# Four narrow projections with the activations moving: 8 or 24 output columns as the stationary operand, turned afterwards

## The chip, the cores and the metric

One core of a Trainium2 chip runs the whole program. The metric is the device time in microseconds of one execution; the figure for a kernel is the median of its runs.

## The reference, cut to what matters

The reference is a stack of three blocks on 512 tokens of width 1024, in fp32. Four of its layers begin with one wide input projection of the normed activations, `u = x @ w_in`, whose columns are then cut into parts: queries, keys, values, gates, and, among them, a few very narrow parts. The narrow ones are the subject here:

- Even layer, `ba`: 8 columns, beta and the decay of a gated delta rule for 4 heads
- Odd layer (here called Fox), `f`: 8 columns, the forget gate of 8 heads
- Second block, `dt` of its state space part (Ssd): 8 columns
- Second block, `gl` of its sparse attention part (Nsa): 24 columns, 3 gates for each of 8 heads

Each is needed with tokens on the partitions: as [128 tokens, 4 token tiles, 8 or 24], that is, 512 x 8 or 512 x 24.

## The kernel before

Activations lie feature-major: 8 tiles of [128 features x 512 tokens], each as a high and a low fp32r half (`Split`), so that a product is three matmuls: high by high, high by low, low by high (`three`, L278). Weights are cut into pieces (`Weights.piece`). SyncE loads them in groups of one or two neighbouring pieces into three raw slots; the load of a group waits until the pieces of the group three places before it have been split. ScalarE copies a piece's high half (`Weights.act`), VectorE subtracts for its low half (`Weights.dve`). Both are called with the key of the piece in use and run one piece ahead: the call for a piece splits also the one that follows in TensorE's order, even where that one belongs to the next layer. The high half of a piece waits until TensorE has finished with the piece two before it.

Two forms of product use a piece. `tile` (L283) keeps 128 (or fewer) weight columns stationary and moves 512 tokens: 8 feature tiles x 3 = 24 matmuls into one PSUM bank, the result with output columns on the partitions. `lin_tm` (L316) keeps 128 tokens of X stationary and moves the weight's columns: for each of 4 token tiles 24 matmuls, so 96, into four banks, the result with tokens on the partitions. The four narrow projections use `lin_tm`. For every matmul there is one load of the stationary operand.

Each engine's order of work is written out by hand. All engines meet at `fence` at the start of a norm and between the stages. `K.rinv`, a [128 x 512] scratch tile, holds a norm's 1/rms and is free once the norm has run.

What stands around the four places:

- Even: 12 qkv tiles, 4 z tiles, `ba`, 8 rope tiles (each followed by one fp32 matmul with the rotation, which waits for ScalarE's copy of the tile), dv. After its split for `ba` ScalarE issues the DMA of the positions (L1091). VectorE copies the four parts of `ba` as they finish, waits for the positions, computes angles for sine and cosine (`rope_tables_dve`), ScalarE applies Sin, and only then copies the first rope tile.
- Fox: the norm, `f` as the first product, 8 q tiles, 8 k tiles, v, 8 gate tiles; `f` is used by VectorE after the gate tiles. The layer ahead of it, `Ple`, ends with 8 proj tiles; for the last of them VectorE calls `G.dve`, which splits the first piece of Fox, and then multiplies and adds the tile into x. The fence of Fox's norm follows.
- Ssd: after a fence `dt`, 8 x tiles (each: ScalarE's copy, a convolution of 4 operations on VectorE, Silu on ScalarE, before ScalarE splits the weights two tiles on), z.
- Nsa: q, k and v tiles, `gl`, on which ScalarE runs a Sigmoid for each of 4 parts, 4 ga tiles with Silu on ScalarE, then the matmuls of a compression (hid) whose results take a Silu too. ScalarE's split call for the last ga tile comes ahead of that tile's Silu and includes the first weights of the output product.

The lines of the helpers in the profile: L90 a matmul, L93 a transpose, L87 a copy, L83 an activation, L96 a tensor_tensor, L99 a tensor_scalar, L102 a scalar_tensor_tensor, L76 the wait in a fence, L255 a weight load's issue.

Of the kernel before, what the change touches and what calls it, by code (L numbers as in the profile page):

```python
# [8 lines left out]
ACT = mybir.ActivationFunctionType  # L9
# [8 lines left out]
    {"ev_pad": 12, "ev_padz": 3, "ev_conv": 12, "ev_qkv": 12, "ev_z": 4, "ev_ba": 4, "ev_y": 1, "ev_na": 1, "ev_beta": 1,  # L18
     "ev_rope": 8, "ev_dv": 4},
# [6 lines left out]
    {"fox_f": 4, "fox_q": 8, "fox_k": 8, "fox_va": 4, "fox_vd": 4, "fox_g": 8, "fox_y": 2, "fox_zero": 5, "fox_lf": 2,  # L26
     "fox_cum": 2},
# [161 lines left out]
class Weights:  # L189
# [453 lines left out]
class Net:  # L643
# [154 lines left out]
def blocks(ap, a):  # L798
    return ap.rearrange("p (a b) -> p a b", a=a)
# [108 lines left out]
class Even:  # L908
# [164 lines left out]
    def act(self, act):  # L1073
        K, G, S = self.K, self.K.G, self.K.S
# [15 lines left out]
        G.act(act, ("even.ba", 0, 0))  # L1090
# [11 lines left out]
        act.wait_ge("ev_ba", 4)  # L1102
# [63 lines left out]
    def dve(self, dve):  # L1166
        K, G, S = self.K, self.K.G, self.K.S
        self.norm.dve(dve)
        cw = K.pv("conv_w")
        for n in range(12):  # L1170
            G.dve(dve, ("even.qkv", n))
            dve.wait_ge("ev_pad", n + 1)
            b, q = self.pads[n % 3], self.qkv[:, n, :]
            dve.own(dve.ts(q, b[:, 0:T], cw[:, n:n + 1], None, MUL, None))
            for j in range(1, 4):
                dve.settle()
                t = dve.stt(q, b[:, j:j + T], cw[:, j * 12 + n:j * 12 + n + 1], q, MUL, ADD)
# [5 lines left out]
        G.dve(dve, ("even.ba", 0, 0))  # L1183
# [15 lines left out]
        dve.wait_ge("ev_ba", 4)  # L1199
# [530 lines left out]
class Fox:  # L1730
# [22 lines left out]
    def pe(self, pe):  # L1753
# [89 lines left out]
    def dve(self, dve):  # L1843
        K, G, S = self.K, self.K.G, self.K.S
        self.norm.dve(dve)
        G.dve(dve, ("fox.f", 0, 0))
        for tt in range(4):
            k = ("fox.f", 0, tt)
            dve.wait_ge("mm", K.done[k])
            dve.cp(self.f[:, tt, :], G.at[k]).then_inc(S("fox_f"), 1)  # L1850
        for n in range(8):
            G.dve(dve, ("fox.q", n))
        for n in range(8):
            k = ("fox.k", n)
# [12 lines left out]
        dve.wait_ge("fox_f", 4)  # L1867
# [79 lines left out]
class Second:  # L1947
# [270 lines left out]
    def ssd_dve(self, dve):  # L2218
# [3 lines left out]
        G.dve(dve, ("ssd.dt", 0, 0))  # L2222
        for tt in range(4):
            k = ("ssd.dt", 0, tt)
            dve.wait_ge("mm", K.done[k])
            dve.cp(self.dt[:, tt, :], G.at[k]).then_inc(S("ssd_dt"), 1)
# [13 lines left out]
        dve.wait_ge("ssd_dt", 4)  # L2240
# [87 lines left out]
class Nsa:  # L2328
# [52 lines left out]
    def pe(self, pe):  # L2381
# [112 lines left out]
    def act(self, act):  # L2494
# [31 lines left out]
        G.act(act, ("nsa.gl", 0, 0))  # L2526
        for tt in range(4):
# [39 lines left out]
    def dve(self, dve):  # L2567
# [29 lines left out]
        G.dve(dve, ("nsa.gl", 0, 0))  # L2597
# [1032 lines left out]
```

## Time and profile before

| | |
|---|---|
| median of 3 runs | 3948.49 us (3943.27 to 3951.49) |
| profiled execution | 3948.09 us, span 3945.8 us |
| mean granted TensorE clock | 0.922 |
| TensorE matmul busy | 3501.7 us, 89% of the span |
| TensorE weight load busy | 2729.1 us, 69% |
| VectorE, ScalarE, GpSimd busy | 52%, 33%, 9% |

The span is the stretch that the profiler's instructions cover; the execution's own time is 2.3 us more. TensorE's busy time is no measure of its speed: matmuls are pipelined, and a matmul that runs at half clock or that waits for its stationary operand's load counts as busy too. The granted clock is given as a share of 2.4 GHz.

### The profile page before, as it was taken

To read this page: it belongs to the slowest core of one execution; us is meant where nothing else is said; L and a number is where in the kernel's file an instruction comes from. 1 tells how busy PE (TensorE), PEld (TensorE's weight loads), DVE (VectorE), ACT (ScalarE), POOL (GpSimd) and SP (SyncE) were. 2 spreads that over 40 slices of the span, in tenths; PEclk is the share of its full clock that TensorE was granted. 3 is DMA by queue.
4 is the path that set the end of the run, shared out by engine and by line. 5 is a ranking of instruction groups with operands and counts; after the bars stand their busy time and mean duration, and the time that the engine had idled before them with its cause. 6 is when DMAs were issued, how large, how long until landed. Compare 5 with 4: busy or idle time off the path is not lost.

```text
span 3945.8 us, 51140 instructions
## 1 busy us (share of the span) xinstructions
PE 3501.7 (89%) x21050; PEld 2729.1 (69%) x21050; DVE 2040.2 (52%) x3597; ACT 1293.1 (33%) x2131; POOL 366.5 (9%) x338
## 2 busy tenths in 40 slices
PE   6977889999899999997797889868888889998998
PEld 4745867777686677775676676546677777776886
DVE  5434446664422456654445425558766773445443
ACT  3222133222222332223333124345455442423321
POOL 0000200000000000000001000025443330000000
PEclk9876989999799999999887989989899989999999
DMA  4210013442343034432201220021111102232321
GB/s 137 59 43 0 1 59 97 138 145 82 64 80 80 24 99 128 139 103 84 91 27 38 60 76 16 27 75 50 36 36 36 47 18 75 65 118 75 97 96 64
DMA packets 318855, 274.93 MB, mean 70 GB/s; under 512 B 10913, under 2 KB 310049, under 8 KB 317857
## 3 DMA queue, kind: packets, MB, share of 16 engines
q1 hardware_dynamic: 314368, 256.07, 22.0%
q10 hardware_dynamic: 4256, 15.59, 1.1%
q8 instruction: 169, 2.77, 0.3%
q14 instruction: 62, 0.50, 0.0%
HBM read 265.35 MB, written 6.29 MB: 69 GB/s over the span
## 4 chain that ended last, share of the span: by engine, by line
PE 75%; DVE 14%; ACT 5%; issue 3%; POOL 1%; DMA 1%; DVEq 0%; ACTq 0%; SPq 0%; POOLq 0%
PE ps L90 73%; DVE f L102 5%; DVE f L96 3%; DVE r L96 2%; ACT f L83 2%; PE ps L93 2%; DVE f L99 2%; DVE f L108 1%; POOL f L96 1%; ACT f L87 1%; ACT r L87 1%; ACT L83 1%; ACT f L84 1%; DVE f L105 0%; DVE f L3173 0%
## 5 line engine op out<-in xcount | busy, mean ns | idle before, releaser
L90 PE MATMUL ps<-r,r 128*128 128x512 f32 (+2 forms) x10656 | 2527.6, 396 | 146.6 <-DVE r L96 100.8
L90 PEld LDWEIGHTS ps<-r,r 128*128 128x128 f32 x10656 | 2003.4, 196 | 624.8 <-issue 192.9
L90 PE MATMUL ps<-f,f 64*64 64x64 f32 (+10 forms) x9458 | 908.9, 283 | 221.3 <-DVE f L96 51.3
L90 PEld LDWEIGHTS ps<-f,f 64*64 64x64 f32 (+4 forms) x9458 | 643.1, 163 | 471.6 <-issue 248.3
L96 DVE TENSOR_TENSOR r<-f,r 128x1024 fp32r<-128x1024 f32 (+2 forms) x619 | 654.1, 1063 | 497.6 <-ACT r L87 490.1
L87 ACT ACTIVATE r<-f 128x1024 fp32r<-128x1024 f32 (+2 forms) x548 | 507.1, 938 | 851.4 <-PE ps L90 715.0
L87 ACT ACTIVATE f<-ps 128x512 f32<-128x512 f32 (+3 forms) x410 | 182.2, 459 | 655.0 <-PE ps L90 416.1
L102 DVE SCALAR_TENSOR_TENSOR f<-f,f,f 128x128 f32<-128x128 f32 (+3 forms) x622 | 362.0, 588 | 41.6 <-ACT f L83 25.6
L96 POOL TENSOR_TENSOR f<-f,f 128x512 f32<-128x512 f32 (+2 forms) x280 | 322.6, 1165 | 517.7 <-ACT f L83 293.3
L96 DVE TENSOR_TENSOR f<-ps,f 128x512 f32<-128x512 f32 (+4 forms) x325 | 178.1, 561 | 330.0 <-PE ps L90 322.3
L83 ACT ACTIVATE f<-ps 128x512 f32<-128x512 f32 (+4 forms) x206 | 112.3, 547 | 658.3 <-PE ps L90 656.4
L96 DVE TENSOR_TENSOR f<-f,f 128x256 f32<-128x256 f32 (+5 forms) x372 | 221.3, 607 | 18.9 <-ACT f L83 10.1
L96 POOL TENSOR_TENSOR r<-f,r 128x512 fp32r<-128x512 f32 (+1 forms) x25 | 38.4, 1537 | 2005.8 <-ACT r L87 2005.8
L96 DVE TENSOR_TENSOR f<-f 128x512 f32<-128x512 f32 x129 | 86.9, 687 | 229.7 <-ACT f L83 217.6
L108 DVE RECIPROCAL f<-f 128x1 f32<-128x1 f32 (+4 forms) x193 | 72.3, 382 | 211.7 <-ACT f L83 105.6
L83 ACT ACTIVATE f<-f 128x512 f32<-128x512 f32 (+8 forms) x206 | 100.3, 514 | 201.3 <-DVE f L102 86.5
L93 PE MATMUL ps<-f,f 128*128 128x128 f32 x552 | 109.3, 319 | 62.4 <-DVE f L102 26.7
L96 DVE TENSOR_TENSOR f<-f,ps 128x512 f32<-128x512 f32 (+1 forms) x192 | 110.8, 594 | 77.5 <-PE ps L90 66.2
L93 PEld LDWEIGHTS ps<-f,f 128*128 128x128 f32 x552 | 72.0, 159 | 86.3 <-DVE f L102 31.8
L87 DVE COPY f<-ps 128x256 f32<-128x256 f32 (+8 forms) x106 | 43.3, 410 | 163.2 <-PE ps L90 156.5
L83 ACT ACT_TABLE_LOAD x89 | 114.2, 1283 | 31.1 <-DVE f L105 18.1
L83 ACT ACTIVATE f<-f,f 128x512 f32<-128x512 f32 (+2 forms) x165 | 109.5, 705 | 14.8 <-POOL f L96 13.9
(32 smaller groups left out, 726.7 us busy)
## 6 DMA issues: line engine op xcount, KB each, us to landing
f<-in_w_mlp_up SPq DMA_DIRECT2D x32, 1024.0 KB, 6.5
f<-in_w_mlp_down SPq DMA_DIRECT2D x32, 1024.0 KB, 6.6
f<-in_w_ff SPq DMA_DIRECT2D x32, 1024.0 KB, 5.3
f<-in_w_ada SPq DMA_DIRECT2D x48, 512.0 KB, 4.1
f<-in_w_in SPq DMA_DIRECT2D x24, 1024.0 KB, 5.3
f<-in_w_in SPq DMA_DIRECT2D x44, 512.0 KB, 3.8
f<-in_w_in_even SPq DMA_DIRECT2D x12, 1024.0 KB, 5.7
f<-in_w_in_odd SPq DMA_DIRECT2D x12, 1024.0 KB, 11.2
```

Of the source, the lines that this page charges most:

```text
L83: return self.e.activation(out, in_, func, bias=bias, scale=scale)
L84: return self.e.activation(out, in_, func, bias=bias, scale=scale, accum_out=acc)
L87: return self.e.activation(out, in_, ACT.Copy) if self.name == "act" else self.e.tensor_copy(out, in_)
L90: return self.e.matmul(out, l, r, start=first, stop=last)
L93: return self.e.transpose(out, in_, ident)
L96: return self.e.tensor_tensor(out, a, b, op)
L99: return self.e.tensor_scalar(out, a, s1, None, o0) if o1 is None else self.e.tensor_scalar(out, a, s1, s2, o0, o1)
L102: return self.e.scalar_tensor_tensor(out=out, in0=a, scalar=s, in1=b, op0=o0, op1=o1)
L108: return self.e.reciprocal(out, in_)
```

## The change

Each of the four narrow projections becomes one `tile` of 24 matmuls with its 8 or 24 weight columns stationary and the 512 tokens moving. The result lies as [8 x 512] or [24 x 512] in one PSUM bank. ScalarE copies it to rows 0 to 7 (0 to 23) of `K.rinv`. TensorE then turns it with four transposes into one bank ([128 x 4 x 8]), and one copy on VectorE (for `gl` one Sigmoid on ScalarE) takes that to its place in SBUF. The transposes are placed behind the tile that follows (for Even behind the first rope tile and its rotation).

Three things move: in Even the DMA of the positions stands behind ScalarE's new wait for the product and its copy; in Fox `f` stands between the q and the k tiles, where it was first; in Nsa the Sigmoid stands behind the four Silus of ga. The counts of semaphores follow.

```diff
+    def turned(self, pe, key, m, landed, drained):
+        K = self.K
+        pe.wait_ge(*landed)
+        b = K.ps.take(pe, drained)
+        for tt in range(4):
+            t = pe.tr(K.ps.t[b][:, tt * m:tt * m + m], K.rinv[0:m, tt * 128:tt * 128 + 128], K.ident[0:m, 0:m])
+        K.mm_done(t, key)
+        return b
...
@@ Even, pe
-        G.lin_tm(pe, "even.ba", W, 2048, 8, X, lambda tt, b: [("ev_ba", tt + 1)])
+        G.tile(pe, "even.ba", W, 2048, 8, X, [("ev_bar", 1)])
         for i in range(8):
             G.tile(pe, ("even.rope", i), ...)
             self.rope.pe(pe, i)
+            if i == 0:
+                self.bank["ba"] = G.turned(pe, "even.baT", 8, ("ev_bar", 1), ("ev_ba", 1))
@@ Even, act
-        G.act(act, ("even.ba", 0, 0))
+        G.act(act, "even.ba")
+        act.wait_ge("mm", K.done["even.ba"])
+        act.cp(K.rinv[0:8, :], G.at["even.ba"]).then_inc(S("ev_bar"), 1)
         act.e.dma_start(self.pos_i, K.A["positions"][0].partition_broadcast(128)).then_inc(S("d_pos"), 16)
@@ Even, dve
-        for tt in range(4):
-            dve.wait_ge("mm", K.done["even.ba", 0, tt])
-            dve.cp(self.ba[:, tt, :], G.at["even.ba", 0, tt]).then_inc(S("ev_ba"), 1)
         dve.wait_ge("d_pos", 16)
...
         for i in range(8):
             G.dve(dve, ("even.rope", i))
+            if i == 0:
+                dve.wait_ge("mm", K.done["even.baT"])
+                dve.cp(self.ba, blocks(K.ps.t[self.bank["ba"]][:, 0:32], 4)).then_inc(S("ev_ba"), 1)
             self.rope.dve(dve, i, ...)
@@ Fox, pe (act and dve follow it)
-        G.lin_tm(pe, "fox.f", W, 4096, 8, X, lambda tt, b: [("fox_f", tt + 1)])
         for n in range(8):
             G.tile(pe, ("fox.q", n), W, n * 128, 128, X, [("fox_q", n + 1)])
+        G.tile(pe, "fox.f", W, 4096, 8, X, [("fox_fr", 1)])
         for n in range(8):
             G.tile(pe, ("fox.k", n), W, 1024 + n * 128, 128, X, [("fox_k", n + 1)])
+            if n == 0:
+                self.bank["f"] = G.turned(pe, "fox.fT", 8, ("fox_fr", 1), ("fox_f", 1))
@@ Ssd, pe (act copies to rinv, dve copies dt at n == 1)
-        G.lin_tm(pe, "ssd.dt", W, 3352, 8, X, lambda tt, b: [("ssd_dt", tt + 1)])
+        G.tile(pe, "ssd.dt", W, 3352, 8, X, [("ssd_dr", 1)])
         for n in range(8):
             G.tile(pe, ("ssd.x", n), ...)
+            if n == 0:
+                self.bank["dt"] = G.turned(pe, "ssd.dtT", 8, ("ssd_dr", 1), ("ssd_dt", 1))
@@ Nsa, pe
-        G.lin_tm(pe, "nsa.gl", W, 1280, 24, X, lambda tt, b: [("nsa_gl", tt + 1)])
+        G.tile(pe, "nsa.gl", W, 1280, 24, X, [("nsa_glr", 1)])
         for n in range(4):
             G.tile(pe, ("nsa.ga", n), ...)
+            if n == 0:
+                self.bank["gl"] = G.turned(pe, "nsa.glT", 24, ("nsa_glr", 1), ("nsa_gl", 1))
@@ Nsa, act
-        for tt in range(4):
-            k = ("nsa.gl", 0, tt)
-            act.wait_ge("mm", K.done[k])
-            act.f(self.gl[:, tt, :], G.at[k], ACT.Sigmoid).then_inc(S("nsa_gl"), 1)
+        act.wait_ge("mm", K.done["nsa.gl"])
+        act.cp(K.rinv[0:24, :], G.at["nsa.gl"]).then_inc(S("nsa_glr"), 1)
         for n in range(4):
             ...
             act.f(self.ga[:, n, :], G.at[k], ACT.Silu).then_inc(S("nsa_ga"), 1)
+        act.wait_ge("mm", K.done["nsa.glT"])
+        act.f(self.gl, blocks(K.ps.t[self.bank["gl"]][:, 0:96], 4), ACT.Sigmoid).then_inc(S("nsa_gl"), 1)
```

## Rows read from the trace of the kernel before

**Rows 1.** The page: the chain of work that ended last, by engine

```profile
PE 75%; DVE 14%; ACT 5%; issue 3%; POOL 1%; DMA 1%; DVEq 0%; ACTq 0%; SPq 0%; POOLq 0%
```

**Rows 2.** Groups by form (busy us, mean ns), two of TensorE, and the page's transposes

```profile
L90 PE MATMUL ps<-r,r 128*128 128x512 f32 x9984 | 2417.9, 401 | 121.8 <-DVE r L96 87.1 <-DVEq L76 17.2 <-ACT r L83 7.2
...
L90 PE MATMUL ps<-r,r 128*128 128x8 f32 x288 | 55.4, 329 | 11.0 <-ACT r L87 9.5 <-DVEq L76 0.9 <-POOL r L96 0.7
...
L93 PE MATMUL ps<-f,f 128*128 128x128 f32 x552 | 109.3, 319 | 62.4 <-DVE f L102 26.7
```

**Rows 3.** Windows, Even: stretch, length, busy and count by engine, granted clock, DMA

```profile
136.03:138.70 2.67, 2.67 (x26) 2.67 (x25) 1.09 (x1) 1.54 (x2) 0.00 (x0) 1.00 0.39 119
...
146.51:151.63 5.12, 5.12 (x25) 5.12 (x26) 0.17 (x1) 0.00 (x0) 0.00 (x0) 0.50 0.00 0
```

**Rows 4.** Timeline, Even: start us, duration, instruction, idle before and releaser

```profile
136.04 0.33 ACTq L1091 DMA_DIRECT2D f<-in_positions  x1
...
151.72 0.42 DVE L87 CAST f<-f 128x512 f32<-128x512 int32 x1
...
162.72 2.07 PE L90 MATMUL ps<-f,f 128*128 128x512 f32 x2 [4.08 <-ACT f L87]
```

**Rows 5.** The positions' two DMAs, from issue to landing

```profile
DMA to landing us min/median/max: 3.1/3.2/3.3
```

**Rows 6.** Timeline at the end of the layer ahead of Fox

```profile
1026.31 97.69 SPq L255 DMA_DIRECT2D f<-in_w_in_odd  x9
...
1029.93 0.26 ACT L87 ACTIVATE r<-f 128x64 fp32r<-128x64 f32 x1 [1.35 <-PE ps L90]
...
1032.40 0.69 DVE L96 TENSOR_TENSOR f<-f,f 128x512 f32<-128x512 f32 x1
```

**Rows 7.** DMA issues, last column landing us; issued near 1028, 1031 and 1080

```profile
f<-in_w_in_odd SPq DMA_DIRECT2D x1, 1024.0 KB, 11.8
...
f<-in_w_in_odd SPq DMA_DIRECT2D x1, 1024.0 KB, 19.7
...
f<-in_w_in_odd SPq DMA_DIRECT2D x1, 1024.0 KB, 8.6
```

**Rows 8.** Timeline at the end of the second such layer: split of the next piece

```profile
1855.62 1.06 ACT L87 ACTIVATE r<-f 128x1024 fp32r<-128x1024 f32 x1 [2.97 <-DMA f<-in_w_mem_kv]
1856.71 1.23 DVE L96 TENSOR_TENSOR r<-f,r 128x1024 fp32r<-128x1024 f32 x1 [1.45 <-ACT r L87]
```

**Rows 9.** Timeline, Fox: last part of X reaches TensorE, and the first read of q0

```profile
1058.47 66.78 PE L90 MATMUL ps<-r,r 128*128 128x8 f32 x287 [0.32 <-POOL r L96]
...
1082.67 0.60 ACT L83 ACTIVATE f<-ps 128x512 f32<-128x512 f32 x1 [6.97 <-PE ps L90]
```

**Rows 10.** Windows, Fox: the second quarter of f, and the tile q1

```profile
1059.33:1064.40 5.07, 5.07 (x25) 5.07 (x26) 0.15 (x3) 0.00 (x0) 1.17 (x3) 0.50 0.01 3
...
1082.67:1088.11 5.44, 5.44 (x25) 4.50 (x24) 1.23 (x1) 1.55 (x2) 0.00 (x0) 1.00 0.35 73
```

**Rows 11.** Timeline, Ssd: start of dt, read of x0, start of x2

```profile
2002.10 31.59 PE L90 MATMUL ps<-r,r 128*128 128x8 f32 x144 [0.88 <-DVEq L76]
...
2028.28 0.60 ACT L87 ACTIVATE f<-ps 128x512 f32<-128x512 f32 x1 [6.83 <-PE ps L90]
...
2034.84 11.38 PE L90 MATMUL ps<-r,r 128*128 128x512 f32 x48 [1.16 <-DVE r L96]
```

**Rows 12.** Nsa: v's last read, window of ga0, table load, wait for output weights

```profile
2267.56 0.28 ACT L87 ACTIVATE f<-ps 128x128 f32<-128x128 f32 x1 [5.08 <-PE ps L90]
...
2284.74:2291.93 7.19, 7.19 (x25) 5.79 (x26) 1.23 (x1) 2.42 (x3) 0.00 (x0) 0.77 0.45 144
...
2285.90 1.28 ACT L83 ACT_TABLE_LOAD   x1
...
2322.01 1.06 ACT L87 ACTIVATE r<-f 128x1024 fp32r<-128x1024 f32 x1 [18.60 <-DMA f<-in_w_out]
```

**Rows 13.** Window in the head norms: 8 stationary, 512 moving columns, fp32

```profile
252.00:254.00 2.00, 2.00 (x5) 0.19 (x4) 0.00 (x0) 1.45 (x3) 0.00 (x0) 1.00 0.00 0
```

More of the change, by code:

```diff
@@ L17 @@
 STAGES = (
-    {"ev_pad": 12, "ev_padz": 3, "ev_conv": 12, "ev_qkv": 12, "ev_z": 4, "ev_ba": 4, "ev_y": 1, "ev_na": 1, "ev_beta": 1,
-     "ev_rope": 8, "ev_dv": 4},
+    {"ev_z": 4, "ev_pad": 12, "ev_padz": 3, "ev_conv": 12, "ev_qkv": 12, "ev_bar": 1, "ev_ba": 1, "ev_y": 1, "ev_na": 1,
+     "ev_beta": 1, "ev_rope": 8, "ev_dv": 4},
     {"diff_elam": 1, "diff_exp": 32, "diff_oa": 8, "diff_pta": 8, "diff_lam": 2, "diff_max": 32, "diff_a": 16, "diff_ptd": 8,
@@ L25 @@
      "gdn_al1": 14, "ev_o": 8},
-    {"fox_f": 4, "fox_q": 8, "fox_k": 8, "fox_va": 4, "fox_vd": 4, "fox_g": 8, "fox_y": 2, "fox_zero": 5, "fox_lf": 2,
-     "fox_cum": 2},
+    {"fox_fr": 1, "fox_f": 1, "fox_q": 8, "fox_k": 8, "fox_va": 4, "fox_vd": 4, "fox_g": 8, "fox_y": 2, "fox_zero": 5,
+     "fox_lf": 2, "fox_cum": 2},
     {"fox_exp": 32, "fox_pt": 32, "fox_row": 8, "fox_max": 32, "fox_r": 32, "fox_n": 32, "fox_out": 8},
@@ L30 @@
      "mem_out": 4},
-    {"ssd_padz": 3, "ssd_pad": 8, "ssd_conv": 8, "ssd_dt": 4, "ssd_z": 4, "ssd_ysum": 1, "ssd_na": 1, "ssd_dta": 1,
-     "ssd_acs": 1, "ssd_dout": 1, "ssd_cdec": 1},
+    {"ssd_dr": 1, "ssd_padz": 3, "ssd_pad": 8, "ssd_conv": 8, "ssd_dt": 1, "ssd_z": 4, "ssd_ysum": 1, "ssd_na": 1,
+     "ssd_dta": 1, "ssd_acs": 1, "ssd_dout": 1, "ssd_cdec": 1},
     {"ssd_xs": 4, "ssd_B": 4, "ssd_Me": 4, "ssd_rms": 4, "ssd_xdt": 4, "ssd_xdd": 4, "ssd_M": 8, "ssd_Mm": 4, "ssd_MM": 8,
      "ssd_y": 8, "ssd_prev": 5, "ssd_yz": 4, "ssd_yn": 4, "ssd_out": 16, "ssd_Mu": 4, "ssd_skip": 4},
-    {"nsa_rk": 2, "nsa_blk": 16, "nsa_ka": 2, "nsa_kd": 2, "nsa_va": 4, "nsa_vd": 4, "nsa_gl": 4, "nsa_ga": 4, "nsa_hid": 4,
-     "nsa_kraw": 1, "nsa_kc": 2, "nsa_hd": 4, "nsa_vbd": 8, "nsa_zero": 4, "nsa_rope": 6},
+    {"nsa_glr": 1, "nsa_rk": 2, "nsa_blk": 16, "nsa_ka": 2, "nsa_kd": 2, "nsa_va": 4, "nsa_vd": 4, "nsa_gl": 1, "nsa_ga": 4,
+     "nsa_hid": 4, "nsa_kraw": 1, "nsa_kc": 2, "nsa_hd": 4, "nsa_vbd": 8, "nsa_zero": 4, "nsa_rope": 6},
     {"nsa_ce": 4, "nsa_exp": 64, "nsa_pt": 68, "nsa_cs": 8, "nsa_cx": 4, "nsa_cn": 4, "nsa_max": 64, "nsa_r": 64, "nsa_n": 64,
@@ L1101, in act @@
             G.act(act, k)
-        act.wait_ge("ev_ba", 4)
+        act.wait_ge("ev_ba", 1)
         act.f(self.beta, self.ba[:, :, 0:4], ACT.Sigmoid).then_inc(S("ev_beta"), 1)
@@ L1182, in dve @@
             G.dve(dve, ("even.z", n))
-        G.dve(dve, ("even.ba", 0, 0))
-        for tt in range(4):
-            dve.wait_ge("mm", K.done["even.ba", 0, tt])
-            dve.cp(self.ba[:, tt, :], G.at["even.ba", 0, tt]).then_inc(S("ev_ba"), 1)
+        G.dve(dve, "even.ba")
         dve.wait_ge("d_pos", 16)
@@ L1198, in dve @@
             dve.cp(self.dv[:, tt, :], G.at["even.dv", 0, tt]).then_inc(S("ev_dv"), 1)
-        dve.wait_ge("ev_ba", 4)
+        dve.wait_ge("ev_ba", 1)
         dve.tt(blocks(self.y, 4), self.ba[:, :, 4:8], blocks(K.pv("dt_bias"), 4), ADD).then_inc(S("ev_y"), 1)
@@ L1802, in act @@
         self.norm.act(act)
-        G.act(act, ("fox.f", 0, 0))
         for n in range(8):
@@ L1808, in act @@
             act.f(self.q[:, n, :], G.at[k], ACT.Copy, scale=128.0 ** -0.5).then_inc(S("fox_q"), 1)
+        G.act(act, "fox.f")
+        act.wait_ge("mm", K.done["fox.f"])
+        act.cp(K.rinv[0:8, :], G.at["fox.f"]).then_inc(S("fox_fr"), 1)
         for n in range(8):
@@ L1845, in dve @@
         self.norm.dve(dve)
-        G.dve(dve, ("fox.f", 0, 0))
-        for tt in range(4):
-            k = ("fox.f", 0, tt)
-            dve.wait_ge("mm", K.done[k])
-            dve.cp(self.f[:, tt, :], G.at[k]).then_inc(S("fox_f"), 1)
         for n in range(8):
             G.dve(dve, ("fox.q", n))
+        G.dve(dve, "fox.f")
         for n in range(8):
@@ L1855, in dve @@
             G.dve(dve, k)
+            if n == 1:
+                dve.wait_ge("mm", K.done["fox.fT"])
+                dve.cp(self.f, blocks(K.ps.t[self.bank["f"]][:, 0:32], 4)).then_inc(S("fox_f"), 1)
             dve.wait_ge("mm", K.done[k])
@@ L1866, in dve @@
             G.dve(dve, ("fox.g", n))
-        dve.wait_ge("fox_f", 4)
+        dve.wait_ge("fox_f", 1)
         dve.tt(self.y, self.f.rearrange("p a b -> p (a b)"), K.pv("b_forget"), ADD).then_inc(S("fox_y"), 1)
@@ L2131, in ssd_act @@
         K, G, S = self.K, self.K.G, self.K.S
-        G.act(act, ("ssd.dt", 0, 0))
+        G.act(act, "ssd.dt")
+        act.wait_ge("mm", K.done["ssd.dt"])
+        act.cp(K.rinv[0:8, :], G.at["ssd.dt"]).then_inc(S("ssd_dr"), 1)
         for n in range(8):
@@ L2221, in ssd_dve @@
         cw, cb = K.pv("conv_w_2"), K.pv("conv_b_2")
[L2222 to L2226, printed above, removed]
+        G.dve(dve, "ssd.dt")
         for n in range(8):
             G.dve(dve, ("ssd.x", n))
+            if n == 1:
+                dve.wait_ge("mm", K.done["ssd.dtT"])
+                dve.cp(self.dt, blocks(K.ps.t[self.bank["dt"]][:, 0:32], 4)).then_inc(S("ssd_dt"), 1)
             dve.wait_ge("ssd_pad", n + 1)
@@ L2239, in ssd_dve @@
             G.dve(dve, k)
-        dve.wait_ge("ssd_dt", 4)
+        dve.wait_ge("ssd_dt", 1)
         dve.tt(self.y, f(self.dt), K.pv("dt_bias_2"), ADD).then_inc(S("ssd_ysum"), 1)
@@ L2525, in act @@
                 act.cp(self.v[m][:, tt, :], G.at[k]).then_inc(S("nsa_va"), 1)
-        G.act(act, ("nsa.gl", 0, 0))
-        for tt in range(4):
-            k = ("nsa.gl", 0, tt)
-            act.wait_ge("mm", K.done[k])
-            act.f(self.gl[:, tt, :], G.at[k], ACT.Sigmoid).then_inc(S("nsa_gl"), 1)
+        G.act(act, "nsa.gl")
+        act.wait_ge("mm", K.done["nsa.gl"])
+        act.cp(K.rinv[0:24, :], G.at["nsa.gl"]).then_inc(S("nsa_glr"), 1)
         for n in range(4):
@@ L2596, in dve @@
                 dve.cp(self.v[m][:, tt, :], G.at[k]).then_inc(S("nsa_vd"), 1)
-        G.dve(dve, ("nsa.gl", 0, 0))
+        G.dve(dve, "nsa.gl")
         for n in range(4):
```

## The prediction

> **What bounds the kernel now.** I read the page first. Its chain of work that ended last is three quarters TensorE [rows 1], so a microsecond taken off TensorE's own list counts where TensorE is what ends last, and only there. I then read the groups by form, to find the instructions that the change touches [rows 2], and then, for each of the four places, the windows (busy time and granted clock) and the timeline. The reader is to see three things. The narrow matmuls have TensorE busy the whole time, with nobody waiting on anything else: in the first place 96 of them fill the stretch from 136.03 to 151.63, 15.60 us. The clock falls inside that stretch: it begins at a granted 1.00, 2.4 GHz, and ends at 0.50, 1.2 GHz, where a quarter of the product takes 5.12 us [rows 3]. And a [128 x 128] by [128 x 512] tile of the same split product, 24 matmuls, takes 5.44 us at full clock [rows 10], whatever it is a tile of.
>
> **What the change removes and adds on TensorE.** Removed: four times 96 matmuls with X as the stationary operand and 8 or 24 moving columns. Added: four times 24 matmuls with 8 or 24 stationary and 512 moving columns, four times four transposes, one ScalarE copy to rinv each, and one copy or sigmoid from PSUM in place of four. The price of 24 matmuls with a narrow stationary operand is not in the trace for this type. The nearest row is the head norms, where an 8-column stationary operand is multiplied with 512 moving columns: five matmul records in 2.00 us at a granted 1.00 [rows 13], 0.4 us each for a plain fp32 product, so it streams by its 512 columns. I take 5.44 us a tile, as for full width; the weight load of 8 columns can only be shorter. Bounds: nothing below some 5 us, and above see the rivals. Four transposes: the row of transposes has a mean of 319 ns for one, latency included [rows 2]; in a row they overlap, so 4 are between 0.4 us and 1.28 us. I take 0.5 us, and 0.9 where the clock is low.
>
> The Trainium skill ("TensorE: Matmul & The Clock Gate", Part 4) puts a transpose at about 275 ns inside a kernel; by that four of them unoverlapped would be 1.1 us and the sum below some 2 us smaller. The row's mean and it are close; neither says how they overlap.
>
> **Place 1, Even.** TensorE finishes the z tiles at 136.03 and the narrow product at 151.63. The next thing that it needs, the first rope matmul at 162.72, waits for the chain of table arithmetic on VectorE that begins with the cast at 151.72 [rows 4]. That chain starts after the last of the four copies. Afterwards the narrow product ends at 136.03 + 5.44 = 141.47. But the positions DMA has moved behind it: before, ScalarE issued it at 136.04, now it issues it after its wait for the product, at 141.5. It takes 3.2 us to land [rows 5]. So the cast starts at 144.7 instead of 151.72: 7.0 us earlier, and the first rope matmul moves with it. Without the DMA's move it would be 10.2; the move costs 3.2 of it. TensorE stands idle from the end of the first rope tile (147) to 155.7 and will be at the low clock there, as it is at 162.72 now (2.07 us for the two rope passes). The transposes follow that matmul at low clock, 0.9 us. Gain 6.1 (4 to 7, by the clock and the transposes).
>
> **Place 2, Fox.** Two effects. First, in the section itself. The last part of X is there at 1058.47. The narrow product comes first now, so it is its first quarter that is paced by the norm; the other three run at the low clock (5.07 us for the second [rows 10]) and q0 ends only when ScalarE reads it, at 1082.67 [rows 9]. Afterwards q0 is paced by the norm and ends 0.7 to 1.3 us after its last operand; with its successor's weights, split by the same steps at the same time, q1 starts at 1059.5. That is 23.2 earlier. Then the f tile is added, 5.44, and the transposes, 0.5: gain 17.2. Second, ahead of the section. The weights of the first Fox piece are split at the end of the layer before, and the code puts that split ahead of the last multiply and add of that layer. Now the piece is f, 32 KB: its DMA goes out at 1026.31, ScalarE splits it at 1029.93, and the last add starts at 1032.40 [rows 6]. After the change the first group is q0 and q1, 1 MB, issued at the same point, since it waits for the same slot. Such a load of this matrix took 11.8 us to land when two more followed it, and 8.6 us later, alone [rows 7]. With 11.8: landed 1038.1, split on ScalarE 1.06 and on VectorE 1.23 [rows 8], multiply and add, layer over at 1041.9 in place of 1033.1. TensorE's norm, behind the fence of all engines, is late by 8.8. The same thing is visible where the second such layer ends: there the next piece is already a 1 MB group and ScalarE sits idle for 2.97 us on that DMA [rows 8]. By that row the delay would be 2.3 (ScalarE was free at 1028.6, so the split would begin at 1031.6 and the rest follow); by 8.6 us of landing 5.6. I take 8.8, because two more loads follow here as they did in the row of 11.8. Net gain 8.4 (7 lower if the load is as slow as a contended later one, 6.5 higher by the mem row).
>
> **Place 3, Ssd.** TensorE starts the narrow product at 2002.10; the next tile, x0, is read at 2028.28, and x2 starts at 2034.84, 6.56 us behind x0's end, by way of ScalarE, the convolution on VectorE and the split [rows 11]. Afterwards x0 ends at 2002.10 + 5.44 + 5.44 = 2013.0, 15.2 earlier. The transposes fall between x0 and x1, and x1 has 1.1 us of room ahead of x2, so they are covered. VectorE's extra copy and the later x1 put some 0.3 us into the convolution chain. Gain 14.9.
>
> **Place 4, Nsa.** The narrow product starts at 2267.56 and the tile behind it ends at 2291.93 [rows 12]. Afterwards 2267.56 + 10.88 = 2278.4: 13.5 earlier, less 0.5 for transposes. Nothing that follows on TensorE waits for anything but its own progress or DMAs that this progress releases, so they move along. But the sigmoid has moved behind the four Silus. ScalarE loads a table between them, 1.28 us [rows 12], which is hidden today. Later ScalarE stands until 2322.01 for the weights of the output product, and does the last Silu of ga and those of hid at once afterwards; TensorE is finished by then and waits for them. The sigmoid now lies in that queue, with a load ahead of it and one behind: 2 x 1.28, and 0.25 for itself (an estimate; the four small ones overlap with nothing either), 2.8 us on the path. Gain 13.0 - 2.8 = 10.2.
>
> The Trainium skill ("ScalarE: Activation LUTs", What ACT_TABLE_LOAD costs) charges 2.66 us for each change of table, load and drain; by that the two would be 5.3 and the gain here 7.4. The row shows 1.28 for the load and no drain of its own.
>
> **The sum.** 6.1 + 8.4 + 14.9 + 10.2 = 39.6 us. The profiled execution took 3948.09 us, 0.4 below the median of 3948.49. 3948.5 - 39.6 = 3908.9, said as 3909.
>
> **The rivals.** (a) The clock falls during the new tile as it falls during the narrow product now. For: it fell there with TensorE busy throughout [rows 3]. Against: in the head norms it stands at 1.00 during matmuls with 8 stationary and 512 moving columns [rows 13]. Price, if it falls as far in as today (some 3.5 us): each tile 1.9 us longer and its successor 1.75 (the tile behind took 7.19 in place of 5.44 [rows 12]), 3.65 x 4 = 15 us: 3924. (b) The q0 group lands soon, as the mem group does: delay 2.3 in place of 8.8, so 3902.5. Against: this matrix's loads are slower in every row. (c) The other side: the narrow tiles do not overlap, each matmul paying its full latency. The row of 8-column stationary operands cannot exclude it at once, since ScalarE paced them. Price: with 0.43 us for each (twice the streaming time, 24 x 0.43 = 10.3) it is 3928. It turns slower than before at (39.6 + 8 + 4 x 5.44) / 96 = 0.72 us a matmul. At 1.0 us it is 3983. Against: full-width ones stream at 0.227, and the array's stream doesn't depend on the stationary width in rows 13. (d) The q0 load eats Fox's whole gain: it would need to land 20.2 us after its issue, and the last of three together took 19.7 [rows 7]; then 3917.
>
> **How the numbers follow.** Forecast as summed, with its own bounds (Even 2, Fox 3, Nsa and Ssd 1 each, and some 4 us between runs): 3902 to 3917, chance 0.67. (b) 0.10, (d) 0.10, (a) 0.09, (c) at some mild price 0.02, above 0.72 us 0.02. The range takes in (b), (d) and most of (a): 3897 to 3925. Measurements of this kernel tell 0.2%, 8 us, from no change: faster 0.96, same 0.02, slower 0.02.
>
> **What would show it.** 24 matmuls of the split type at full clock in each place, ending 5.4 us after their start, except in Fox, where they run between q7 and k0. The granted clock near 1.00 where it is 0.50 now. The positions DMA issued at about 141.5 and the cast right after its landing. At the end of the layer before Fox, ScalarE idle some 8 to 10 us with the odd matrix's DMA as releaser and the norm's start near 1043. In Nsa two table loads right after the Silu of ga. It is wrong if the clock falls in the new tiles, if q0's weights land much earlier or later than 1038, or if one of the transposes' copies holds TensorE up.

## The result, and the profile after

The changed kernel takes 3907.82 us (median of 4 runs, 3902.29 to 3909.26) against 3945.89 for the kernel before beside it: 38.1 us less, ratio 0.9903, 95% interval 0.9888 to 0.9918. The forecast was 3909 us, and faster with a chance of 0.96. The profiled execution is the fastest of the four, 3902.29 us.

The page of the kernel after: its span, TensorE's busy time, the chain by engine, and the largest group of matmuls.

```profile
span 3899.7 us, 50586 instructions
...
PE 3445.0 (88%) x20778; PEld 2657.7 (68%) x20778; DVE 2039.2 (52%) x3588; ACT 1295.9 (33%) x2133; POOL 366.1 (9%) x338
...
PE 75%; DVE 14%; ACT 5%; issue 3%; DMA 1%; POOL 1%; DVEq 0%; ACTq 0%; SPq 0%; POOLq 0%
...
L90 PE MATMUL ps<-r,r 128*128 128x512 f32 x10368 | 2468.5, 397 | 143.5 <-DVE r L96 99.3
```

TensorE is busy 56.7 us less than before (3501.7) and still ends the chain [rows 1]. The windows of the four new tiles, in the order Even, Fox, Ssd, Nsa, answer to [rows 3, 10]:

```profile
136.56:142.09 5.53, 5.53 (x25) 2.31 (x24) 1.23 (x1) 1.54 (x2) 0.00 (x0) 1.00 0.04 14
1093.31:1098.84 5.53, 5.53 (x25) 2.31 (x24) 1.22 (x1) 1.54 (x2) 0.00 (x0) 1.00 0.99 106
...
1983.40:1989.10 5.70, 5.70 (x25) 2.36 (x26) 1.22 (x1) 1.04 (x1) 0.18 (x3) 1.00 0.01 1
...
2232.01:2237.54 5.53, 5.53 (x25) 2.61 (x24) 1.23 (x1) 1.22 (x2) 0.00 (x0) 1.00 0.00 0
```

Each has 24 matmuls at a granted 1.00. Three are over in 5.53 us; Ssd's, which starts from a fence, takes 5.7. The weight loads (the second engine column) are busy 2.3 to 2.6 us, where the 96 of before kept them busy the whole time [rows 3].

Where did the time go? SyncE issues the same loads in the same order in both kernels, so its issue times are landmarks: the distance between two of them is the time of what lies between. In us:

| stretch (from issue to issue) | before | after | difference | forecast |
|---|---|---|---|---|
| Even: first load to w_out_even | 220.0 | 213.2 | -6.8 | -6.1 |
| first attention: to w_mlp_up | 327.7 | 323.0 | -4.7 | 0 |
| Fox: w_in_odd to w_out_odd | 195.2 | 187.8 | -7.5 | -8.4 |
| second attention: to w_mlp_up | 146.4 | 149.2 | +2.8 | 0 |
| Ssd: w_in to w_cmp_k | 333.1 | 316.2 | -16.9 | -14.9 |
| Nsa: w_cmp_k to the next w_in | 278.9 | 268.6 | -10.3 | -10.2 |

Four places: 41.5 us. Fox's stretch begins at the issue of the late load, so its wait is in it. The two attention stretches (1.9 us together) and all the others (2.7) make up the rest of the 46.1 us between the two spans; what the attention stretches do is taken up with after_again.

The timelines hold the steps. Even, the kernel after:

```profile
142.09 0.59 ACT L87 ACTIVATE f<-ps 8x512 f32<-8x512 f32 x1 [3.99 <-PE ps L90]
142.10 0.34 ACTq L1105 DMA_DIRECT2D f<-in_positions  x1
145.31 0.43 DVE L87 CAST f<-f 128x512 f32<-128x512 int32 x1 [5.94 <-DMA f<-in_positions]
...
156.32 2.08 PE L90 MATMUL ps<-f,f 128*128 128x512 f32 x2 [8.83 <-ACT f L87]
...
158.33 0.59 PE L93 MATMUL ps<-f,f 8*128 8x8 f32 x4
```

z3, the last z tile, is read at 136.56. From there to the cast it is 8.75 us, in place of 15.69 [rows 4], and to the rope matmul 19.76 in place of 26.69. The cast now waits for the positions, and TensorE comes to the rope matmuls at the low clock (2.08 us for two) and turns the result there, in 0.59 us for the four transposes.

Fox, the kernel after: the load of the first pair, its split, the norm's start, and q0's first read; then the narrow tile, the turning and the copy behind it.

```profile
1012.43 4.46 SPq L255 DMA_DIRECT2D f<-in_w_in_odd  x3
...
1023.96 1.06 ACT L87 ACTIVATE r<-f 128x1024 fp32r<-128x1024 f32 x1 [9.26 <-DMA f<-in_w_in_odd]
...
1028.74 2.05 PE L90 MATMUL ps<-f,f 128*128 128x512 f32 x2 [10.99 <-DVE f L96]
...
1054.82 0.60 ACT L83 ACTIVATE f<-ps 128x512 f32<-128x512 f32 x1 [1.86 <-PE ps L90]
...
1098.84 0.59 ACT L87 ACTIVATE f<-ps 8x512 f32<-8x512 f32 x1 [3.99 <-PE ps L90]
...
1104.17 0.41 PE L93 MATMUL ps<-f,f 8*128 8x8 f32 x4
...
1106.57 0.18 DVE L87 COPY f<-ps 128x32 f32<-128x32 f32 x1
```

The load lands 11.5 us after its issue (1023.96 - 1012.43), ScalarE having stood 9.26 us on it, and the norm starts 16.31 us after the issue, where before it was 1034.24 - 1026.31 = 7.93: 8.38 us late.

Ssd, the kernel after: the copy of the narrow tile, the turning, x0's read.

```profile
1989.15 0.59 ACT L87 ACTIVATE f<-ps 8x512 f32<-8x512 f32 x1 [4.71 <-PE ps L90]
...
1994.51 0.41 PE L93 MATMUL ps<-f,f 8*128 8x8 f32 x4
1994.62 0.60 ACT L87 ACTIVATE f<-ps 128x512 f32<-128x512 f32 x1 [3.93 <-PE ps L90]
```

The section starts at 1983.40, so x0 is read after 11.22 us; before it was 26.18 [rows 11]. Nsa, the kernel after, where ScalarE's wait for the output weights ends:

```profile
2272.08 1.06 ACT L87 ACTIVATE r<-f 128x1024 fp32r<-128x1024 f32 x1 [17.02 <-DMA f<-in_w_out]
2273.05 0.58 ACT L83 ACTIVATE f<-ps 128x512 f32<-128x512 f32 x1
...
2273.64 1.28 ACT L83 ACT_TABLE_LOAD   x1
...
2274.94 0.25 ACT L83 ACTIVATE f<-ps 128x96 f32<-128x96 f32 x1
2275.21 1.28 ACT L83 ACT_TABLE_LOAD   x1
2276.50 0.56 ACT L83 ACTIVATE f<-ps 128x62 f32<-128x62 f32 x4
2276.94 1.89 PE L90 MATMUL ps<-f,f 128*128 128x32 f32 x8 [2.83 <-ACT f L83]
```

The sigmoid stands between two table loads, and TensorE waits 2.83 us behind them.

### The profile page after: what moved, and what is told of

The parts are those of the page before. It is cut to its first block, busy times and chain, and to the rows that moved or that the text cites. A ratio compares the mean times of both kernels' runs of the same rounds, so it can differ in the third digit from the quotient of the medians.

```text
span 3899.7 us, 50586 instructions
## 1 busy us (share of the span) xinstructions
PE 3445.0 (88%) x20778; PEld 2657.7 (68%) x20778; DVE 2039.2 (52%) x3588; ACT 1295.9 (33%) x2133; POOL 366.1 (9%) x338
## 4 chain that ended last, share of the span: by engine, by line
PE 75%; DVE 14%; ACT 5%; issue 3%; DMA 1%; POOL 1%; DVEq 0%; ACTq 0%; SPq 0%; POOLq 0%
PE ps L90 73%; DVE f L102 5%; DVE f L96 3%; DVE r L96 3%; PE ps L93 2%; ACT f L83 2%; DVE f L99 2%; DVE f L108 1%; ACT r L87 1%; ACT f L87 1%; POOL f L96 1%; ACT L83 1%; ACT f L84 1%; DVE f L3195 0%; DVE f L105 0%
## 5 line engine op out<-in xcount | busy, mean ns | idle before, releaser
L90 PE MATMUL ps<-r,r 128*128 128x512 f32 x10368 | 2468.5, 397 | 143.5 <-DVE r L96 99.3
L90 PEld LDWEIGHTS ps<-r,r 128*128 128x128 f32 x10368 | 1931.9, 191 | 632.4 <-issue 193.6
L87 ACT ACTIVATE f<-ps 128x512 f32<-128x512 f32 (+3 forms) x414 | 184.6, 460 | 669.5 <-PE ps L90 424.7
L96 DVE TENSOR_TENSOR f<-ps,f 128x512 f32<-128x512 f32 (+4 forms) x325 | 178.1, 561 | 327.7 <-PE ps L90 320.1
L83 ACT ACTIVATE f<-ps 128x512 f32<-128x512 f32 (+3 forms) x203 | 111.9, 553 | 636.3 <-PE ps L90 634.5
L93 PE MATMUL ps<-f,f 128*128 128x128 f32 (+2 forms) x568 | 110.9, 316 | 63.3 <-DVE f L102 29.3
L93 PEld LDWEIGHTS ps<-f,f 128*128 128x128 f32 (+2 forms) x568 | 73.4, 159 | 90.3 <-DVE f L102 34.0
L83 ACT ACTIVATE f<-f,f 128x512 f32<-128x512 f32 (+2 forms) x165 | 109.5, 705 | 14.9 <-POOL f L96 13.9
L102 DVE SCALAR_TENSOR_TENSOR f<-ps,f,f 128x512 f32<-128x512 f32 x48 | 36.0, 751 | 146.2 <-PE ps L90 141.5
```

Source lines behind the costliest of these rows:

```text
L83: return self.e.activation(out, in_, func, bias=bias, scale=scale)
L87: return self.e.activation(out, in_, ACT.Copy) if self.name == "act" else self.e.tensor_copy(out, in_)
L90: return self.e.matmul(out, l, r, start=first, stop=last)
L93: return self.e.transpose(out, in_, ident)
L96: return self.e.tensor_tensor(out, a, b, op)
L102: return self.e.scalar_tensor_tensor(out=out, in0=a, scalar=s, in1=b, op0=o0, op1=o1)
```

## The experiments

Two questions. Why is the narrow product cheaper with the activations moving: is it the clock, or the 24 matmuls in place of 96? And are the three waits that the change brought (q0's load, the positions, the sigmoid) worth what the forecast took off for them? "Before" and its ratio are always from the same chip as the run; the differences to the kernel after are against its first median, 3907.82 us.

**wide.** The kernel before, with its few weight columns repeated along the moving operand, so that each of the 96 matmuls streams 128 columns (120 where there are 24). Only the first 8 or 24 are read.

```
+ ww = w * (128 // w)
+ wh = wh.unsqueeze(1).broadcast_to((128, 128 // w, w))
- self.three(pe, ps[:, 0:w], X.hi, X.lo, hi[:, q, :], lo[:, q, :], ...)
+ self.three(pe, ps[:, 0:ww], X.hi, X.lo, wh, wl, ...)
```

> The kernel before, with the moving operand of the four narrow projections repeated to 128 columns (8 columns 16 times, 24 columns 5 times): the same 96 matmuls with the same 96 weight loads each, but up to 16 times the moving columns; only the first 8 or 24 result columns are used. Theory (what the change gained is to a large part the clock, which falls during the narrow product): with 128 moving columns the clock stays at 1.00 as it does in the v tiles of Nsa (24 matmuls of that form in 2.68 us), so a product takes 10.7 us and the tile after it 5.44. Even 4.9 less, Fox 9.9 (three quarters 15.3 to 8.0, q0 8.0 to 5.4), Ssd 10.0, Nsa 8.2: 33 us less than before, near 3913, in spite of more work. Rival (the 96 weight loads set the time and the clock has nothing to do with it): quarters stay at 5.12 us and the kernel at 3946.

3927.3 us (3925.07 to 3939.62) against 3949.49, ratio 0.9957 (0.9942 to 0.9972): between the two. The windows of wide show why. They are a quarter in Even, one in Fox, the first and the second in Ssd, and most of Nsa's.

```profile
136.00:138.60 2.60, 2.60 (x26) 2.60 (x25) 1.13 (x1) 1.43 (x2) 0.00 (x0) 1.00 0.46 104
...
1050.30:1055.30 5.00, 5.00 (x25) 5.00 (x25) 0.13 (x1) 0.00 (x0) 1.09 (x3) 0.50 0.00 0
...
2260.20:2267.80 7.60, 7.60 (x70) 7.60 (x70) 0.00 (x0) 0.57 (x3) 0.00 (x0) 1.00 0.00 0
```

```profile
1995.30:1998.30 3.00, 3.00 (x25) 3.00 (x26) 1.23 (x1) 0.95 (x1) 0.10 (x3) 0.90 0.00 0
1998.50:2003.40 4.90, 4.90 (x25) 4.90 (x25) 0.01 (x1) 0.00 (x0) 0.00 (x0) 0.50 0.01 3
```

In Even and in Nsa the quarters take 2.6 to 2.7 us: the same 96 weight loads, at the full clock. In Fox, where the tile comes to the low clock, and in Ssd, where the clock falls some 2.5 us in, the later quarters take 5.12 us, as the slow ones did before [rows 3, 10]. A quarter at the full clock is 24 weight loads of 0.11 us, and the weight loads are busy throughout. So both theories hold a part: at the full clock the 96 cost 10.7 us, the 24 of the change 5.5; at the low clock 20.5.

By the stretches, the wide form alone gives 6.1 us in Even, 0.9 in Fox, 3.1 in Ssd and 7.6 in Nsa, 17.7 in all: in Even nearly as much as the change, in Fox and Ssd little. The medians differ by 22.2. Part of the rest doesn't belong to the narrow tiles at all: behind the four places, from the issue of the first load of the last w_in group to that of w_conv_pw, where the instructions are the same, wide took 822.0 us and wide_late 822.2, and every other profile, before and after, 828.1 to 828.5. Why is open.

**wide_late.** The same, with Fox's narrow tile behind its q tiles and Ssd's behind its x tiles.

```
  # Fox.pe; Ssd likewise, ScalarE's and VectorE's lists with them
- G.lin_tm(pe, "fox.f", W, 4096, 8, X, ...)
  for n in range(8):
      G.tile(pe, ("fox.q", n), W, n * 128, 128, X, ...)
+ G.lin_tm(pe, "fox.f", W, 4096, 8, X, ...)
```

> The kernel with 128 moving columns in the narrow tiles (3927.3 us, where the quarters of Even and Nsa took 2.68 us and those of Fox and Ssd 5.12), with Fox's narrow tile behind its q tiles and Ssd's behind its x tiles, so that each follows dense tiles at the full clock. If what TensorE did before decides whether such a tile keeps the full clock, the quarters take 2.68 us in both places: 9.8 us less in Fox and 7.8 in Ssd, about 3910 us. Rival: something of these two places themselves holds the clock down, the quarters stay at 5.12 us and the time near 3927.

The quarters take 2.68 us in Fox. Timeline of wide_late, VectorE's four reads, and a window between them:

```profile
1096.58 0.16 DVE L87 COPY f<-ps 128x8 f32<-128x8 f32 x1
1099.17 0.17 DVE L87 COPY f<-ps 128x8 f32<-128x8 f32 x1 [2.43 <-PE ps L90]
1101.85 0.17 DVE L87 COPY f<-ps 128x8 f32<-128x8 f32 x1 [2.51 <-PE ps L90]
1104.53 0.17 DVE L87 COPY f<-ps 128x8 f32<-128x8 f32 x1 [2.51 <-PE ps L90]
```

```profile
1099.30:1101.80 2.50, 2.50 (x25) 2.50 (x24) 0.04 (x1) 0.00 (x0) 0.00 (x0) 1.00 0.96 295
2048.10:2050.40 2.30, 2.30 (x23) 2.30 (x23) 1.02 (x3) 0.00 (x0) 0.00 (x0) 1.00 0.22 23
```

In both places the clock stays at 1.00 now, so the layer itself holds nothing down: what differs is what ran on TensorE just before. Ssd's stretch is 10.4 us shorter than in wide (319.6 for 330.0; 7.8 forecast). The time, though, was 3920.47 us (ratio 0.9932, 0.9908 to 0.9957), only 6.8 below wide, and Fox's stretch only 2.0 shorter. The profiled execution is the fastest of the four; its span is 12.9 us below that of wide. The norm's start in wide, and then in wide_late, shows where most of Fox's 9.8 went:

```profile
1025.35 8.57 PE L90 MATMUL ps<-f,f 128*128 128x512 f32 x16 [2.60 <-DVE f L96]
```

```profile
1029.35 9.56 PE L90 MATMUL ps<-f,f 128*128 128x512 f32 x16 [10.98 <-DVE f L96]
```

Against their issues of w_in_odd (1017.44 and 1013.05) these are 7.91 and 16.30 us. With q0 first, the small tile isn't there to be split while the 1 MB load lands, and 8.4 us are lost, here without any turned tile. My expectation (3910 us) had left this out: a miss of mine, and the cleanest proof of the step. A further 3.9 us went between the second w_mlp_up and Ssd's first load, 556.3 us for 552.4; no run shows by what.

**fox_first.** The kernel after with Fox's turned tile ahead of q0 again, its transposes behind q0.

```
+ G.tile(pe, "fox.f", W, 4096, 8, X, [("fox_fr", 1)])
  for n in range(8):
      G.tile(pe, ("fox.q", n), W, n * 128, 128, X, ...)
+     if n == 0: self.bank["f"] = G.turned(pe, "fox.fT", 8, ...)
- G.tile(pe, "fox.f", W, 4096, 8, X, [("fox_fr", 1)])
```

> The changed kernel with f moved back ahead of the q tiles, still as one tile of 24 matmuls; the transposes behind q0. Theory (the wait of ScalarE for q0's load at the end of the layer ahead delays everything): the first piece is the 32 KB one again, the wait of 9.26 us goes, the norm's matmuls start 8.7 us earlier; in the section itself the same nine tiles run in another order, so the whole gain stays: 3899. Rival (the wait is hidden, since the same load would be waited for a little later): no change, 3908.

3901.44 us, ratio 0.9881 (0.9865 to 0.9897), 6.4 below the kernel after; its Fox stretch is 178.5 for 187.8, 9.2 less (7.9 less than in after_again). I had expected 3899; 1.9 us of the difference lie in its Ssd stretch, see below. The norm starts 7.93 us after the issue again (1029.19 - 1021.26), and the narrow tile is the one that the norm paces:

```profile
1029.19 8.80 PE L90 MATMUL ps<-f,f 128*128 128x512 f32 x16 [2.60 <-DVE f L96]
1044.96 5.28 PE L90 MATMUL ps<-r,r 128*8 128x512 f32 x12 [6.97 <-ACT r L87]
```

**fox_undo** and **ssd_undo.** The kernel after, with the class of Fox, or Ssd's three lists, taken from the kernel before. Fox's part in TensorE's list:

```
- G.tile(pe, "fox.f", W, 4096, 8, X, ...); G.turned(pe, "fox.fT", 8, ...)
+ G.lin_tm(pe, "fox.f", W, 4096, 8, X, lambda tt, b: [("fox_f", tt + 1)])
```

> The kernel after with Fox's eight columns done as before, alone. The prediction's term for Fox, 17.2 less 8.8 of waiting for q0's load, says 8.4 us more than the kernel after: 3916 us. The shift of the issue times between the two profiles says 7.5: 3915 us. Rival: the late load eats the whole gain of the place, then 3908.

> The kernel after with Ssd's eight columns done as before, alone. The prediction's term says 14.9 us more than the kernel after: 3923 us. The shift of the issue times says 16.9: 3925 us. Rival: part of that shift came from the quarter tiles of the attention ahead, which differ from one execution to the next, then 13 or less: 3921 or below.

fox_undo: 3912.16 us (3909.08 to 3915.49; 3915 to 3916 expected), ratio 0.9914 (0.9891 to 0.9937). That is 4.3 above the first runs of the kernel after, and the spreads overlap, so the time alone doesn't settle this term. Its Fox stretch does: 194.5 us against 187.8 and, in after_again, 186.4, so 6.7 to 8.1 us, and the norm starts 7.93 us after the issue. ssd_undo: 3923.8 us (3915.66 to 3927.38), ratio 0.9934 (0.9912 to 0.9956), 16.0 above; its Ssd stretch is 333.15 us, that of before 333.13, and every run with the turned tile ahead of x0 lies at 316.1 to 316.2, but for fox_first with 318.1. The rivals (the whole gain of Fox lost; 13 or less in Ssd) are out.

**pos_early.** The kernel after with the positions' DMA issued ahead of ScalarE's wait for the narrow tile.

```
+ act.e.dma_start(self.pos_i, positions)
  act.wait_ge("mm", K.done["even.ba"])
  act.cp(K.rinv[0:8, :], ...)
- act.e.dma_start(self.pos_i, positions)
```

> The changed kernel with the DMA of the positions issued ahead of ScalarE's wait for the narrow product, as before the change. By the prediction's own step the move of the DMA costs its landing of 3.2 us, so 3.2 less. By the trace of the changed kernel VectorE no longer waits for the product itself at all (its four copies are gone), so the cast starts as soon as the DMA has landed or VectorE has split the weights of the first rope tile: near 139.8 in place of 145.3, 5.5 us less, and TensorE's wait ahead of the first rotation falls from 8.8 to about 3.3. 3902.3 against 3904.6; the timeline tells which.

3903.71 us (3901.33 to 3905.01), ratio 0.9887 (0.9871 to 0.9903), 4.1 below; the spread overlaps with that of the kernel after, so the stretch and the timeline decide here too: the Even stretch is 6.8 us shorter. Its timeline:

```profile
135.65 0.34 ACTq L1103 DMA_DIRECT2D f<-in_positions  x1
138.82 0.43 DVE L87 CAST f<-f 128x512 f32<-128x512 int32 x1 [0.37 <-DMA f<-in_positions]
149.84 1.24 PE L90 MATMUL ps<-f,f 128*128 128x512 f32 x2 [3.27 <-ACT f L87]
```

The cast doesn't wait for the narrow tile at all: it starts 3.2 us after the issue, with the tile half done. The rope matmul comes 14.2 us after z3's read, not 19.8.

**sig_early.** The kernel after with Nsa's sigmoid ahead of the Silu of ga1.

```
  for n in range(...):   # ga
      G.act(act, k)
+     if n == 1: act.wait_ge("mm", K.done["nsa.glT"]); act.f(self.gl, ..., ACT.Sigmoid)
      act.wait_ge("mm", K.done[k]); act.f(self.ga[:, n, :], ..., ACT.Silu)
- act.wait_ge("mm", K.done["nsa.glT"]); act.f(self.gl, ..., ACT.Sigmoid)
```

> The changed kernel with the Sigmoid of gl placed after ScalarE's split call for ga1, ahead of its wait for ga1, where it is idle for 4.5 us; the two table loads go with it. Theory (the two table loads and the Sigmoid lie on the path behind the wait for the output weights): the first matmul of the compressed keys starts 2.8 us earlier, 3905. Rival (TensorE's own matmuls of the compression end last there): no change.

3905.77 us (3904.89 to 3906.46), ratio 0.9893 (0.9877 to 0.9909), 2.0 below, which by itself shows nothing; the Nsa stretch is 3.7 us shorter (264.9 for 268.6). That is 0.9 more than the two loads and the sigmoid (2.8). Windows of the matmuls behind that wait, in the kernel after and then in sig_early:

```profile
2276.94:2278.80 1.86, 1.86 (x8) 1.75 (x8) 0.00 (x0) 0.13 (x2) 0.00 (x0) 0.50 0.77 271
```

```profile
2279.50:2280.95 1.45, 1.45 (x13) 1.35 (x12) 0.86 (x1) 0.65 (x5) 0.00 (x0) 1.00 0.88 307
```

After standing 2.83 us, TensorE comes back at the low clock, where 8 matmuls take 1.86 us, 0.23 each; without the wait the clock is full, and the 13 matmuls of that window take 1.45, 0.11 each.

**best.** Fox's turned tile ahead of q0, the sigmoid early, and in Even the positions' DMA ahead of the z tiles with the rotary tables made before either engine waits for the narrow tile.

> The kernel after with three waits taken away: Fox turns its narrow tile ahead of q0 (alone 6.4 us less than the kernel after), the rotary tables are made before ScalarE and VectorE wait for the narrow tile of Even (the transfer's move alone gave 4.1, and the tables' work off the path should give 2 to 3.5 more), and Nsa's Sigmoid comes before the second wait of ScalarE for w_out (alone 2.0). If the three waits lie one behind another on one path, they add up: 12.5 to 16 below the kernel after, 3892 to 3895 us. Rival: the time freed in front of a load of weights is waited for at that load, so that a part is lost: 3898 or more.

3887.7 us (3887.4 to 3888.61), ratio 0.9852 (0.983 to 0.9874): 20.1 below the kernel after, more than the 12.5 to 16 expected. Place by place it is 9.5 in Even, 9.2 in Fox and 3.7 in Nsa, 22.5 in all, while its profiled execution had the longer of the first attention stretches (327.6). The three waits do add up. No single run has Even's part alone in this form. In Even the tables are ready while the narrow tile runs:

```profile
131.92 0.42 DVE L87 CAST f<-f 128x512 f32<-128x512 int32 x1
...
141.98 0.59 ACT L87 ACTIVATE f<-ps 8x512 f32<-8x512 f32 x1 [0.52 <-PE ps L90]
...
148.48 1.13 PE L90 MATMUL ps<-f,f 128*128 128x512 f32 x2 [0.69 <-ACT f L87]
149.54 0.41 PE L93 MATMUL ps<-f,f 8*128 8x8 f32 x4
```

TensorE goes through at the full clock: two rope matmuls in 1.13 us, four transposes in 0.41.

**after_again.** The changed kernel, once more.

> The kernel after, timed again in five rounds. Its four places, added up from the issue times that mark them in the profiles, give 40 to 42 us less than before, 0.9895; the four first runs gave a median 38.1 us less. If the two stretches of attention, whose clock differs between executions of one and the same program, are what moves a single execution, the runs spread over 5 us or more and the median lies at 3904 to 3909 us. Rival: some place holds more than the issue times showed, and the median lies outside that.

3910.71 us (3910.6 to 3914.41) against 3948.67, ratio 0.9909 (0.9892 to 0.9925): 38.0 less, above the range that I gave for its median but the same difference as at first. All eight runs of the kernel after have a median of 3909.9. In its profile the four places are 42.6 us below before (6.5, 8.8, 17.0 and 10.3), but its first attention stretch is 327.4 us, as before, and not 323.0; the same program gave both. Windows of that stretch, first in the kernel after, then in fox_first, which has the same instructions up to there:

```profile
273.94:293.94 20.00, 11.98 (x48) 6.98 (x48) 10.02 (x44) 6.16 (x22) 0.00 (x0) 0.67 0.00 0
293.94:313.94 20.00, 12.93 (x46) 7.83 (x46) 9.57 (x41) 5.87 (x20) 0.00 (x0) 0.59 0.01 1
```

```profile
275.43:295.43 20.00, 13.89 (x47) 8.04 (x47) 9.52 (x40) 5.92 (x20) 0.00 (x0) 0.50 0.00 0
295.43:315.43 20.00, 13.89 (x46) 8.05 (x46) 9.65 (x40) 5.76 (x20) 0.00 (x0) 0.50 0.00 1
```

The granted clock differs, and with it the stretch; in after_again it is 0.50 in both windows (274.26 to 314.26). Why one execution gets the one and another the other isn't shown. Whether a run meets the one or the other moves it by nearly 5 us. The second attention stretch took 149.1 to 151.8 us in all ten profiles taken since and 146.4 in the one of before, so 2.8 to 5.4 us of the four places' gain are missing there; fox_undo, whose Fox is that of before, has 149.2 and wide, without any turned tile, 149.1, so it isn't Fox's turned tile that gives it back. Whether the profile of before was one lucky execution isn't settled: it is the only one of that kernel. Together: 46.1 us between two single spans, 38 between medians.

## Why the prediction was right

The sum was 39.6 us; the four places hold 41.5 in the profile, the medians differ by 38. That the time itself came within 1.2 us is in part luck: the kernel before ran 2.6 us below the median that the sum started from, and what the places gave beyond the forecast was lost again elsewhere. By its steps:

- **The tile.** 5.44 us forecast, 5.53 measured in three places and 5.7 in Ssd, at a granted 1.00 in all four. Rival (a), that the clock falls in it, is out, and so is (c), at 0.23 us for a matmul. The 3.5 us after which (a) had the clock fall were one place's: in the kernel before it fell 5.0 us into the narrow product in Even, 3.4 in Nsa and 2.6 in Ssd. The four transposes in a row took 0.41 to 0.43 us at the full clock and 0.59 at the low one, so 0.5 and 0.9 in the sum were a little high. The Trainium skill ("TensorE: Matmul & The Clock Gate", Part 4) has about 275 ns for one transpose in a kernel, measured on 128 x 128 in bf16. Four of those apart would be 1.1 us, an estimate; the four of this trace, 8 x 128 or 24 x 128 in fp32, overlap.
- **Even, 6.1.** Cast 6.94 us earlier (7.0 forecast), rope matmul 6.93, stretch 6.8. Wrong was the aside that the DMA's move costs 3.2 of it: pos_early got back 5.6 us at the rope matmul. I had let the cast wait for the end of the tile, which it doesn't need.
- **Fox, 8.4.** Both halves hold. The late load costs 8.38 us, 8.0 in after_again (8.8 forecast, 11.5 us of landing for 11.8), shown in after, fox_undo, fox_first and wide_late. The section gives 15.6 to 17.4 us: from the norm's start to the end of the last of the nine groups 70.1 us, and 69.2 in after_again, against 85.7 in fox_undo and 86.5 before. The forecast without its transposes was 17.7. Net, by the stretches against fox_undo, 6.7 to 8.1. Rivals (b) and (d) are out: the load lands neither soon nor after 20 us.
- **Ssd, 14.9.** From the section's start to the first transpose of its scan it is 84.99 us for 99.72, 14.7 less; the scan then takes 67.3 us in both. The other 2.1 of the stretch come behind it, in two tiles in which the clock is on its way up: 48 matmuls take 13.04 us in place of 14.05, and 24 take 7.35 in place of 8.45. The granted clock of the first 7 us of the former is 0.71 after and 0.56 before. ssd_undo has before's values again (14.06 and 8.41), and six profiles with the turned tile lie at 12.96 to 13.05 and 7.29 to 7.36. But fox_first, which has the turned tile too, has 13.42 and 8.09, and wide, with 96 matmuls there, 12.77 and 7.33. So the turned tile doesn't decide it alone, these 2.1 us are not shown to be its doing, and what brings them stays open.
- **Nsa, 10.2.** The tiles give 13.4 (10.99 for 24.37 us from v's last read to ga0's), 13.0 forecast. The sigmoid costs 3.7, not 2.8, because TensorE stands and then runs at the low clock. That leaves 9.7, and the stretch has 10.3; the 0.6 between them isn't placed. For a change of table the Trainium skill ("ScalarE: Activation LUTs", What ACT_TABLE_LOAD costs) has 2.66 us with the drain. Both loads here are 1.28 us long, the first starts 0.01 us behind the Silu, and the sigmoid starts 0.02 us behind it, so this trace shows the load and no drain.

Also open is why the narrow product loses the clock. With 8 or 24 moving columns it fell from 1.00 even behind dense tiles (Even, Nsa), with 128 or 120 it stayed there and fell only behind sparse work (Ssd); a rule for it isn't shown.

## What to carry to other kernels

In this kernel a product with few output columns was cheaper with these columns stationary and the activations moving: 24 matmuls of 0.23 us in place of 96 weight loads, a full clock where it had mostly been half, and some half a microsecond for turning the result back. But the narrow tile did hidden work where it was: being small it was split while the next megabyte landed, so it is better left first. And look at what stood behind it in each engine's list: a DMA issued after its wait, tables that never needed it, a sigmoid between two Silus. The sigmoid, the tables and Fox's first tile, moved, gave 20 us more on a change that had brought 38.

## What was not expected of the hardware

- With X stationary, 8 and 128 moving columns cost the same at the low clock, 5.12 us for 24 matmuls: the weight loads set the pace there, and at the full clock too (2.68).
- A tile of 96 such matmuls with 128 or 120 moving columns kept the clock that it came in with (Even, Nsa: 1.00; Fox: 0.50) or lost it (Ssd, 2.5 us in), though TensorE was busy throughout; none got it back.
- A stall of 2.8 us on TensorE cost nearly 1 us more (3.7 us in the stretch) by the lower clock after it.
- One program took 323.0 or 327.4 us for the same attention stretch, at a granted clock of 0.67 and 0.59, or of 0.50, in a part of it.
